# mLSTM steps as one pipelined step each, every second projection group, with PSUM bank 3 taken from the projections

## Chip, cores and metric

The kernel runs on one core of a Trainium2 chip. The metric is the device time of one execution in microseconds (us), the median of several runs. In the profile the engines are PE (matrix products), DVE, ACT, POOL (elementwise) and SP (it issues DMAs). PSUM, where PE writes and DVE and ACT read, has eight banks of 128 partitions x 512 float32.

## What is computed

One layer of a hybrid backbone over 512 latent tokens and 128 context tokens, width 1024: normalised and modulated tokens go through one wide input projection, whose columns feed three branches (neighbourhood attention, 8 heads of 64; a bidirectional mLSTM, 4 heads of 128; a gated short convolution); the branches are projected, gated, merged, and a SwiGLU feed-forward follows. The part that the change rewrites is the chunked mLSTM. For each chunk of 128 tokens, direction and head:

```
inter = b + m;  mt = max(inter, max(d));  w_int = exp(inter - mt)
s   = (q @ k.T) * exp(d - mt)                     # scores times decay
num = w_int * (q @ C) + s @ v                     # state product + score product
den = w_int * (q @ n) + sum(s)
h   = num / max(abs(den), exp(-mt))
C, n = decay * C + (wk * k).T @ v,  decay * n + sum(wk * k)
```

Attention is `softmax(q @ k.T + bias) @ v`, the projections are `h @ w_in`.

## The kernel before

Every large product is computed to float32 accuracy from float32r halves: each operand is split into a high part (ACT copies it with rounding, L1239 and its like) and a low part (DVE subtracts, L1699), and `three` (L2386 to L2390) issues three products for each 128-row slice of the contraction. So PE runs one long stream of products, in *groups*. A group fills one PSUM bank with the sum over the contraction: 24 products of 320 columns for the units q, k, mq, cc, cx, cb, gate and mo, 12 for a branch unit (br), and for mk and mv 24 products of 512 columns in four *parts* of 6. ACT or DVE then *drains* the bank, and PE may start the next group on that bank when its previous user is drained (`bank_free`, L2378).

The order of everything is a list, `PLAN`, which `make_plan` (L193) writes once; each engine walks the list in order and issues what it has to do at each step, with semaphore waits. Three things stand in that list besides the groups:

- `split` steps: for a block of weights ACT makes the high part and DVE the low part; the block's slot must first have been released by the group or part that read its previous content. Blocks of the unit `ada` are no product operands: DVE multiplies them with the condition rows in the same place (L1713).
- `side` lists: small work that is put between the groups. In `unit` (L235) one entry is taken at each of the four groups j of a unit (at j 0 and 2 alone in a br unit, other than the last), one more at j = 1 in q, k and mq units; for mk and mv (L409) an entry is taken at parts 0 and 2, and at all four parts of the last token tile. What is left at the unit `mif` is put out at once (L395), just ahead of the group `kout`, which turns the context keys.
- The side work is first attention, ten steps `na` of two units each (nine pairs; the last pair is of context heads). Step 0 of a pair: PE scores of this pair and value products of the last; DVE adds the bias, takes the maximum. ACT exponentiates the first unit in step 0, the second in step 1, where DVE divides. Step 2: PE transposes the probabilities (L2672), ACT copies them out (L1573), and the next step 0 multiplies with the values (L2657, L2661); DVE writes the result (L2107, L2110). Then the mLSTM: 20 steps `ml` of two heads (4 of the context, 16 of the latent chunks).

An ml step has two halves. `("ml", 0, n)`: PE broadcasts the row of `mpair` (L2701) and, at the first visit of a chunk and head pair, computes the scores (L2710); DVE forms the exponent (L2229), ACT scales the keys (L1609) and exponentiates (L1613), DVE multiplies (L2236). `("ml", 1, n)`, one group later: PE multiplies scores with values (L2722), queries with the state (L2724), keys with values (L2726), and turns the keys that the next first visit needs (`turn_keys`, L2528, L2536); ACT scales the state product (L1618), DVE sums and updates the state (L2244 to L2255) and normalises (L2262 to L2272). The ml steps use banks 4 to 7, called `A[0]` to `A[3]`; the projections use banks 0 to 3 in turn, but 0 to 2 from the first k unit until mif (`three_banks`), since attention keeps its value products in bank 3.

Ahead of the mLSTM stand, at units cc and cx, the steps mstat, mscan, mnat, mexp and mcols: running sums and maxima of the gates, some 23 us of small DVE operations that begin with the drain of kout (L1770) and end at L2207 and L2215. At mcols PE transposes the results (L2681), sums the chunk ends (L2685), and waits for DVE's copies of them (L2132 to L2135, semaphore `ms_rd`) before it turns the first keys:

```
                    pe.wait_ge(ms_rd, 3)
                    pe.wait_ge(act_drain, drains("A", gid("mk", 0, TT - 1)))
                    turn_keys(0)
```

After the last br unit of this stage (`("br", (2, 3))`) come eight mo groups, then products by a seven-product scheme (`wu` steps), whose sums, splits and operands DVE and ACT prepare. The feed-forward begins in the same way: `tsum` is four sums on DVE (L2305 to L2311, semaphore `ts_done` 5 to 8), and `tsplit` 0 to 3 split their results (ACT L1640, DVE L2317):

```
                    if j == 0:
                        act.wait_ge(x1_out, 16 * TT)
                        act.wait_ge(ts_done, 8)
```

Of the kernel before, what the change touches and what calls it, by code (L numbers as in the profile page):

```python
# [18 lines left out]
ALU = mybir.AluOpType  # L19
# [3 lines left out]
P = 128  # L23
# [169 lines left out]
def make_plan():  # L193
# [41 lines left out]
    def unit(n):  # L235
        kind, which = UNITS[n][:2]
        for j, emit in enumerate(tiles(n)):
# [14 lines left out]
            if side and (kind != "br" or j % 2 == 0 or UNITS[n][:2] == ("br", (2, 3))):  # L252
                plan.extend(side.pop(0))
# [137 lines left out]
    while UNITS[n][0] != "out":  # L391
        kind, which = UNITS[n][0], UNITS[n][1]
        if kind != "ada":
            if kind == "mif":
# [3 lines left out]
                three_banks[0] = False  # L398
# [88 lines left out]
    plan += [("tsum",), ("tsplit", 0)]  # L487
    ff_group("fg", 0, 0, 1)
    plan += [("tsplit", 1), ("wsum", NG)]
# [154 lines left out]
def program(nc, a, out, vline, gline, xline, gdram):  # L644

    ctx = ExitStack()
    with ctx:
# [279 lines left out]
        def _(sp):  # L927
# [42 lines left out]
            for step in PLAN:  # L970
# [50 lines left out]
                elif step[0] == "ml" and step[1] == 1 and ML_UNITS[step[2]][0] == CH:  # L1021
                    n = step[2]
# [195 lines left out]
        def _(act):  # L1218
# [48 lines left out]
            def drain(g):  # L1267
# [122 lines left out]
            def turned_keys(n):  # L1390
# [5 lines left out]
                nc.scalar.activation(kt, A[2][:, 0:256].rearrange("p (i t) -> p i t", i=2), ACT.Copy).then_inc(kt_rd, 1)  # L1396
# [81 lines left out]
            for step in PLAN:  # L1478
# [115 lines left out]
                elif step[0] == "ml":  # L1594
                    _, sub, n = step
                    ch, dr, hp, first, last = ML_UNITS[n]
                    b = n % 2
                    if sub == 0:
# [3 lines left out]
                        if SCORES[ch, hp][0] == n:  # L1602
                            nc.scalar.activation(scores[:, scores_held(ch, hp)],
                                                 A[1][:, 0:256].rearrange("p (i t) -> p i t", i=2),
                                                 ACT.Copy).then_inc(ml_sc, 1)
                        for i in range(2):
                            r = dr * 4 + 2 * hp + i
                            hd = 2 * hp + i
                            ins = nc.scalar.activation(kw_sb[:, b, i, :], mk[:, ch, hd * P:(hd + 1) * P], ACT.Copy,  # L1609
                                                       scale=mcols[:, ch, 2, r:r + 1])  # L1610
                        ins.then_inc(ml_kw, 1)
                        act.wait_ge(ml_dm, n + 1)
                        nc.scalar.activation(e_sb[:, b], e_sb[:, b], ACT.Exp, scale=-1.0).then_inc(ml_e, 1)  # L1613
                    if sub == 1 and ch < CH:
                        act.wait_ge(ml_b, n + 1)
# [5 lines left out]
                    if sub == 1 and n + 1 in FIRST_VISITS:  # L1621
# [64 lines left out]
        def _(dve):  # L1686
# [213 lines left out]
            def ada5_block(j):  # L1900
# [7 lines left out]
                ins.then_inc(ada5_done, 1)  # L1908

# [62 lines left out]
            for step in PLAN:  # L1972
# [248 lines left out]
                elif step[0] == "ml":  # L2221
                    _, sub, n = step
                    ch, dr, hp, first, last = ML_UNITS[n]
                    b = n % 2
                    if sub == 0:
                        dve.wait_ge(ml_a, n + 1)
                        for i in range(2):
                            r = dr * 4 + 2 * hp + i
                            ins = nc.vector.scalar_tensor_tensor(e_sb[:, b, i, :], A[0][:, i * P:(i + 1) * P],  # L2229
                                                                 mcols[:, ch, 0, r:r + 1], mask_m[:, dr, :],  # L2230
                                                                 ALU.subtract, ALU.max)
                        ins.then_inc(ml_dm, 1)
                        dve.wait_ge(ml_e, n + 1)
                        first_n = SCORES[ch, hp][0]
                        dve.wait_ge(ml_sc, sum(1 for v in SCORES.values() if v[0] <= first_n))
                        nc.vector.tensor_tensor(st_sb[:, b], scores[:, scores_held(ch, hp)], e_sb[:, b],  # L2236
                                                ALU.mult).then_inc(ml_st, 1)
                    else:
                        dve.wait_ge(ml_b, n + 1)
                        intra = A[3][:, 0:258].rearrange("p (i e) -> p i e", i=2)  # L2240
                        upd = A[1][:, 0:258].rearrange("p (i e) -> p i e", i=2)
# [620 lines left out]
```

## Time and profile before

| | |
|---|---|
| runs | 1126.8, 1127.04, 1125.51 us; median 1126.8 |
| profiled execution, own time | 1128.61 us |
| its span, first to last instruction | 1126.8 us |
| PE busy | 1105.7 us, 98% of the span |
| DVE, ACT, POOL busy | 790.6, 515.9, 90.6 us |
| mean granted PE clock | 0.996 of 2.4 GHz |
| HBM | 125 GB/s over the span |

Times in the rows are from the span's start. In a timeline a row is: start, duration, engine, line, operation, output<-inputs, shape, count, and in brackets the idle time just before it with what ended it. The ends of products are modelled and overlap the next ones, so what one costs is the distance from its start to the next start.

### The profile page before, as it was taken

The numbers are of one execution on the slowest core, as the hardware profiler recorded it, in microseconds if no ns is written. First come the engines' busy times: TensorE is split into PE (matmuls) and PEld (weight loads), VectorE is DVE, ScalarE is ACT, GpSimd is POOL, SyncE is SP. The second block draws the span as 40 slices with busy tenths as digits, with TensorE's granted clock in tenths as the row PEclk, the third lists the DMA queues.
The fourth block names the chain that finished last, engine by engine and source line by source line (L and its number), as shares of the span: only waits on it lengthen the run. The fifth ranks groups of instructions, "written<-read, shape, count | busy, mean of one in ns | idle before, by whom it ended". The sixth has DMA issues, their size and how long they took to land.

```text
span 1126.8 us, 18487 instructions
## 1 busy us (share of the span) xinstructions
PE 1105.7 (98%) x7136; PEld 1038.9 (92%) x7136; DVE 790.6 (70%) x1405; ACT 515.9 (46%) x965; POOL 90.6 (8%) x149
## 2 busy tenths in 40 slices
PE   6999999999999999999999999999999999999997
PEld 4799998789999999999999988999999999988886
DVE  5748978768675666888868637999987777633444
ACT  5534443434334333355553238555555555533431
POOL 2052322000000000210100003000000000000002
PEclk9999999998999999999999999999999999999999
DMA  9675563452531122035466345053422232425112
GB/s 361 237 233 166 182 197 90 145 144 81 83 68 57 57 72 61 20 101 181 145 222 225 120 128 179 18 168 127 149 77 76 87 139 75 125 67 183 57 38 93
DMA packets 42918, 141.78 MB, mean 126 GB/s; under 512 B 9392, under 2 KB 10960, under 8 KB 41168
## 3 DMA queue, kind: packets, MB, share of 16 engines
q1 hardware_dynamic: 38752, 131.64, 36.4%
q0 software_dynamic: 4080, 8.97, 2.5%
q8 instruction: 57, 0.93, 0.4%
q14 instruction: 29, 0.24, 0.1%
HBM read 127.93 MB, written 12.60 MB: 125 GB/s over the span
## 4 chain that ended last, share of the span: by engine, by line
PE 92%; DVE 4%; ACT 2%; issue 1%; DMA 1%; SPq 0%; POOL 0%; POOLq 0%; ACTq 0%; DVEq 0%
PE ps L2388 28%; PE ps L2390 28%; PE ps L2389 28%; PE ps L2657 1%; PE ps L2672 1%; PE ps L2722 1%; PE ps L2631 1%; PE ps L2724 1%; PE ps L2726 1%; DMA xt<-in_x_sample 1%; DVE w_lo L1699 1%; PE ps L2598 0%; PE ps L2446 0%; PE ps L2710 0%; PE ps L2632 0%
## 5 line engine op out<-in xcount | busy, mean ns | idle before, releaser
L2390 PE MATMUL ps<-h_hi,w_lo 128*128 128x320 f32 x960 | 297.6, 310 | 0.0
L2389 PE MATMUL ps<-h_lo,w_hi 128*128 128x320 f32 x800 | 248.3, 310 | 0.0
L2388 PE MATMUL ps<-h_hi,w_hi 128*128 128x320 f32 x736 | 232.1, 315 | 1.3 <-ACT mo L1336 0.8
L2390 PEld LDWEIGHTS ps<-h_hi,w_lo 128*128 128x128 f32 x960 | 181.2, 189 | 0.0
L2388 PE MATMUL ps<-w_hi,h_hi 128*128 128x512 f32 x418 | 164.8, 394 | 0.0
L2390 PE MATMUL ps<-w_hi,h_lo 128*128 128x512 f32 x418 | 162.8, 390 | 0.0
L2389 PE MATMUL ps<-w_lo,h_hi 128*128 128x512 f32 x418 | 162.8, 389 | 0.0
L2389 PEld LDWEIGHTS ps<-h_lo,w_hi 128*128 128x128 f32 x800 | 151.3, 189 | 0.1
L2388 PEld LDWEIGHTS ps<-h_hi,w_hi 128*128 128x128 f32 x736 | 139.3, 189 | 2.9 <-issue 2.2
L1699 DVE TENSOR_TENSOR w_lo<-raw,w_hi 128x1024 fp32r<-128x1024 f32 x93 | 112.5, 1222 | 40.3 <-ACT w_hi L1239 39.7
L1239 ACT ACTIVATE w_hi<-raw 128x1024 fp32r<-128x1024 f32 x93 | 96.6, 1052 | 65.3 <-PE ps L2390 60.3
L2388 PE MATMUL ps<-h_hi,w_lo 128*128 128x320 f32 x336 | 104.4, 311 | 0.8 <-ACT snap L1377 0.8
L2388 PE MATMUL ps<-tt_hi,w_hi 128*128 128x320 f32 x336 | 103.8, 309 | 0.0
L2389 PE MATMUL ps<-tt_lo,w_hi 128*128 128x320 f32 x336 | 103.8, 309 | 0.0
L2390 PE MATMUL ps<-tt_hi,w_hi 128*128 128x320 f32 x336 | 103.8, 309 | 0.0
L2389 PE MATMUL ps<-h_lo,w_lo 128*128 128x320 f32 x336 | 103.8, 309 | 0.0
L2388 PEld LDWEIGHTS ps<-w_hi,h_hi 128*128 128x128 f32 x418 | 78.5, 188 | 18.3 <-issue 2.1
L2390 PEld LDWEIGHTS ps<-w_hi,h_lo 128*128 128x128 f32 x418 | 78.5, 188 | 16.4
L2389 PEld LDWEIGHTS ps<-w_lo,h_hi 128*128 128x128 f32 x418 | 78.5, 188 | 15.7
L1746 DVE TENSOR_TENSOR h_lo<-ff,h_hi 128x1280 fp32r<-128x1280 f32 (+1 forms) x22 | 30.5, 1428 | 64.4 <-ACT h_hi L1264 64.4
L1830 DVE TENSOR_TENSOR w_hi<-raw,w_hi 128x512 fp32r<-128x512 f32 x84 | 58.0, 690 | 22.9 <-ACT w_hi L1368 22.8
L2388 PEld LDWEIGHTS ps<-h_hi,w_lo 128*128 128x128 f32 x336 | 63.1, 188 | 1.3 <-issue 1.2
(313 smaller groups left out, 2030.6 us busy)
## 6 DMA issues: line engine op xcount, KB each, us to landing
raw<-in_w_blocks SPq DMA_DIRECT2D x182, 512.0 KB, 3.9
ada<-in_w_first SPq DMA_DIRECT2D x8, 1024.0 KB, 20.2
gdram<-stage SPq DMA_DIRECT2D x8, 640.0 KB, 6.6
gt<-gdram SPq DMA_DIRECT2D x8, 640.0 KB, 5.8
xline<-x SPq DMA_DIRECT2D x5, 512.0 KB, 5.3
x<-xline SPq DMA_DIRECT2D x5, 512.0 KB, 7.7
xt<-in_x_sample SPq DMA_DIRECT2D x4, 512.0 KB, 6.4
condr<-in_cond_rows POOLq DMA_DIRECT2D x2, 1024.0 KB, 8.1
```

Source lines behind the costliest of these rows:

```text
L1239: ins = nc.scalar.activation(held(w_hi, b), raw[:, s, :], ACT.Copy)
L1699: nc.vector.tensor_tensor(held(w_lo, b), raw[:, s, :], held(w_hi, b).bitcast(F32), ALU.subtract).then_inc(lo_done, 1)
L1746: nc.vector.tensor_tensor(h_lo[:, o2 + k:o2 + k + n, :], ff[:, k0 + k:k0 + k + n, :], h_hi[:, o2 + k:o2 + k + n, :].bitcast(F32), ALU.subt ...
L1830: nc.vector.tensor_tensor(v[:, 512:1024], summand(w, q), v[:, 0:512].bitcast(F32), ALU.subtract).then_inc(flo_done, 1)
L2388: nc.tensor.matmul(dst, wh, xh, start=first, stop=False, skip_group_check=resumed)
L2389: nc.tensor.matmul(dst, wh, xl, start=False, stop=False, skip_group_check=resumed)
L2390: return nc.tensor.matmul(dst, wl, xh, start=False, stop=last, skip_group_check=resumed)
L2631: nc.tensor.matmul(dst[:, 0:256], q, kk, start=True, stop=True)
L2657: ins = nc.tensor.matmul(dst[:, 0:P], src, pt[:, b, i, c * P:(c + 1) * P], start=(c == 0), stop=(c == 2))
L2672: ins = nc.tensor.transpose(A[2 * b + i][:, c * P:(c + 1) * P], sx[:, b, i, c * P:(c + 1) * P], ident)
L2722: ins = nc.tensor.matmul(A[3][:, pr], st_sb[:, b, i, :], mv[:, ch, hd, :], start=True, stop=True)
L2724: ins = nc.tensor.matmul(A[0][:, pr], mq[:, hd, tok(ch)], cl[:, r, :], start=True, stop=True)
```

## The change

- The two halves of neighbouring ml steps are put together. `("ml", n)` for n = 0 to 20 holds, on PE, the turning of the next keys, the broadcast and scores of step n (`ml_scores`), then the products of step n - 1 (`ml_values`); on DVE the exponent of n, the state update of n - 1 (`ml_state`), the score product of n, the sum and normalisation of n - 1 (`ml_sum`); on ACT the parts that go with them.
- Broadcast, scores and turned keys get banks of their own: A[2] for the broadcast, bank 3 for scores and turned keys. For that the projections use three banks until the mo groups.
- One entry of `side` is taken at groups 0 and 2 of a unit (0 alone in a br unit other than the last) in place of every group.
- At mcols the first keys are turned ahead of the small transposes, and PE no longer waits there for `ms_rd`.
- In the feed-forward, tsplit 1 comes before tsplit 0, and each waits for its own sum, not for all four.
- The mo drains wait for `ml_b`, the last products, in place of `ml_h`, the last normalisation.

```
@@ make_plan
-            if side and (kind != "br" or j % 2 == 0 or UNITS[n][:2] == ("br", (2, 3))):
+            if side and (j == 0 or kind != "br" and j == 2 or UNITS[n][:2] == ("br", (2, 3)) and j == 2):
                 plan.extend(side.pop(0))
...
                 for s in side:
                     plan.extend(s)
                 side = []
-                three_banks[0] = False
                 group("kout", n)
...
             elif kind == "mo" and which == 0:
                 assert not side
+                three_banks[0] = False
                 gate_stretch()
...
             for s in range(len(ML_UNITS)):
-                side += [[("ml", 0, s)], [("ml", 1, s)]]
+                side.append([("ml", s)])
+            side.append([("ml", len(ML_UNITS))])
...
-    plan += [("tsum",), ("tsplit", 0)]
+    plan += [("tsum",), ("tsplit", 1)]
     ff_group("fg", 0, 0, 1)
-    plan += [("tsplit", 1), ("wsum", NG)]
+    plan += [("tsplit", 0), ("wsum", NG)]
@@ ACT
-                    act.wait_ge(ml_h, len(ML_UNITS))
+                    act.wait_ge(ml_b, len(ML_UNITS))
...
-                    if j == 0:
+                    if j == 1:
                         act.wait_ge(x1_out, 16 * TT)
-                        act.wait_ge(ts_done, 8)
+                    act.wait_ge(ts_done, (7, 5, 8, 6)[j])
@@ DVE
+                        ins.then_inc(ml_dm, 1)
+                    if n:
+                        ml_state(n - 1)
+                    if n < len(ML_UNITS):
...
                                                 ALU.mult).then_inc(ml_st, 1)
+                    if n:
+                        ml_sum(n - 1)
@@ PE
+            def ml_scores(n):
+                ch, dr, hp, _, _ = ML_UNITS[n]
+                if n:
+                    pe.wait_ge(ml_dm, n)
+                else:
+                    pe.wait_ge(ms_rd, 3)
+                    pe.wait_ge(stat_rd, 1)
+                    pe.wait_ge(pair_rd, 1)
...
+            def ml_values(n):
...
+                pe.wait_ge(ml_st, n + 1)
+                pe.wait_ge(ml_kw, n + 1)
+                if n:
+                    pe.wait_ge(ml_c, n)
...
                 elif step[0] == "mcols":
+                    turn_keys(0)
                     pe.wait_ge(stat_rd, 2)
...
-                    pe.wait_ge(ms_rd, 3)
-                    pe.wait_ge(act_drain, drains("A", gid("mk", 0, TT - 1)))
-                    turn_keys(0)
                 elif step[0] == "ml":
+                    if step[1] + 1 in FIRST_VISITS:
+                        turn_keys(step[1] + 1)
+                    if step[1] < len(ML_UNITS):
+                        ml_scores(step[1])
+                    if step[1]:
+                        ml_values(step[1] - 1)
```

What the order becomes, engine by engine, at three places.

PE at the end of mv, before the change (the last products of mv, then kout's transposes; the last attention products came ten parts of mv earlier):

```order
L2388 MATMUL ps<-w_hi,h_hi 128x512
L2389 MATMUL ps<-w_lo,h_hi 128x512
L2390 MATMUL ps<-w_hi,h_lo 128x512
L2388 MATMUL ps<-w_hi,h_hi 128x512
L2389 MATMUL ps<-w_lo,h_hi 128x512
L2390 MATMUL ps<-w_hi,h_lo 128x512
L2474 MATMUL ps<-cst,nak 128x128 x4
L2388 MATMUL ps<-h_hi,w_hi 128x320
```

and now (L2731 transposes the last pair's probabilities, L2720 multiplies them with the values, L2488 is kout):

```order
L2404 MATMUL ps<-w_hi,h_lo 128x512
L2402 MATMUL ps<-w_hi,h_hi 128x512
L2403 MATMUL ps<-w_lo,h_hi 128x512
L2404 MATMUL ps<-w_hi,h_lo 128x512
L2731 MATMUL ps<-cst,sx 128x128 x8
L2720 MATMUL ps<-pt,vctx 64x128 x8
L2488 MATMUL ps<-cst,nak 128x128 x4
L2402 MATMUL ps<-h_hi,w_hi 128x320
```

The last steps of attention, which had products of mv behind them, stand with none between each other and kout.

ACT in the same place, before (L1562 exponentiates, L1310 drains mv, L1573 copies the transposed probabilities, L1239 splits weights, L1577 belongs to mstat):

```order
L1573 ACTIVATE pt<-ps 128x768 x2
L1562 ACTIVATE sx,small<-sx,small 128x128 x4
L1310 ACTIVATE mv<-ps 128x4x128
L1562 ACTIVATE sx,small<-sx,small 128x128 x4
L1310 ACTIVATE mv<-ps 128x4x128
L1573 ACTIVATE pt<-ps 128x2x256 x2
L1310 ACTIVATE mv<-ps 128x4x128 x2
L1239 ACTIVATE w_hi<-raw 128x1024 x2
L1310 ACTIVATE mv<-ps 128x4x128
L1239 ACTIVATE w_hi<-raw 128x1024
L1577 ACTIVATE stat_114<-stat_113 36x640
```

and now (L1563, L1311, L1574, L1240 and L1578 are the same operations):

```order
L1574 ACTIVATE pt<-ps 128x768 x2
L1563 ACTIVATE sx,small<-sx,small 128x128 x4
L1240 ACTIVATE w_hi<-raw 128x1024
L1563 ACTIVATE sx,small<-sx,small 128x128 x4
L1240 ACTIVATE w_hi<-raw 128x1024
L1311 ACTIVATE mv<-ps 128x4x128
L1240 ACTIVATE w_hi<-raw 128x1024
L1574 ACTIVATE pt<-ps 128x2x256 x2
L1578 ACTIVATE stat_114<-stat_113 36x640
```

A split has come between the two units' exponentials, and two splits and the last drain of mv stand directly ahead of the copy of the probabilities.

PE at mcols, before (last transposes of the gate statistics, the sum of chunk ends, the first keys, then the group cx):

```order
L2681 MATMUL ps<-cst,ib 128x36
L2681 MATMUL ps<-cst,lf 128x36
L2681 MATMUL ps<-cst,stat_114 128x36
L2681 MATMUL ps<-cst,stat_119 128x36
L2685 MATMUL ps<-ends,parity 128x32
L2536 MATMUL ps<-cst,mk 128x128 x2
L2388 MATMUL ps<-h_hi,w_hi 128x320
```

and now (the first keys, L2554, ahead of the transposes):

```order
L2402 MATMUL ps<-h_hi,w_hi 128x320
L2403 MATMUL ps<-h_lo,w_hi 128x320
L2404 MATMUL ps<-h_hi,w_lo 128x320
L2554 MATMUL ps<-cst,mk 128x128 x2
L2741 MATMUL ps<-cst,ib 128x36
L2741 MATMUL ps<-cst,lf 128x36
L2741 MATMUL ps<-cst,stat_114 128x36
L2741 MATMUL ps<-cst,stat_119 128x36
L2741 MATMUL ps<-cst,ib 128x36
```

The keys' transposes have left the place behind L2685.

## Rows read from the trace of the kernel before

**Rows 1.** The page: busy time of PE.
```profile
PE 1105.7 (98%) x7136; PEld 1038.9 (92%) x7136; DVE 790.6 (70%) x1405; ACT 515.9 (46%) x965; POOL 90.6 (8%) x149
```
**Rows 2.** Waits of PE, whole span: total us, times, longest.
```profile
PE ps L2598 <- DVE xt L1983: 9.2, 2, 8.3
...
PE ps L2388 <- ACT snap L1377: 0.8, 1, 0.8
```
**Rows 3.** Timeline of PE: the last attention pair, then kout.
```profile
210.41 1.26 PE L2635 MATMUL ps<-nak,naq 64*128 64x128 f32 x16
...
213.07 0.50 PE L2388 MATMUL ps<-w_hi,h_hi 128*128 128x512 f32 x1
...
221.39 1.03 PE L2672 MATMUL ps<-cst,sx 128*128 128x128 f32 x8
...
225.10 1.09 PE L2661 MATMUL ps<-pt,vctx 128*64 128x128 f32 x16
...
239.86 0.60 PE L2474 MATMUL ps<-cst,nak 128*128 128x128 f32 x4
240.80 0.39 PE L2388 MATMUL ps<-h_hi,w_hi 128*128 128x320 f32 x1 [0.34 <-ACT mv L1310]
```
**Rows 4.** Timeline of PE: the last but one pair, in the last tile of mk.
```profile
197.78 0.71 PE L2631 MATMUL ps<-nak,naq 64*128 64x256 f32 x4
...
205.95 0.52 PE L2672 MATMUL ps<-cst,sx 128*128 128x128 f32 x3 [0.73 <-DVE sx L2122]
```
**Rows 5.** Timeline of ACT, same place: a split between the pair's two exponentials.
```profile
202.62 1.06 ACT L1239 ACTIVATE w_hi<-raw 128x1024 fp32r<-128x1024 f32 x1 [0.57 <-PE ps L2390]
203.59 0.60 ACT L1562 ACTIVATE sx<-sx,small 128x384 f32<-128x384 f32 x1
```
**Rows 6.** Timeline of DVE: a low part; last pair's division; its output.
```profile
203.72 1.23 DVE L1699 TENSOR_TENSOR w_lo<-raw,w_hi 128x1024 fp32r<-128x1024 f32 x1 [0.76 <-ACT w_hi L1239]
...
218.65 0.87 DVE L2122 TENSOR_SCALAR sx<-sx,small 128x128 f32<-128x128 f32 x4
...
226.24 0.76 DVE L2110 COPY att<-ps 128x256 f32<-128x256 f32 x2 [4.31 <-PE ps L2661]
```
**Rows 7.** Timeline of ACT: first and last of the last unit's exponentials; copy of its probabilities.
```profile
216.70 0.39 ACT L1562 ACTIVATE sx<-sx,small 128x128 f32<-128x128 f32 x1
...
218.14 0.19 ACT L1562 ACTIVATION_READ_ACCUMULATOR sx<-sx,small 128x1 f32 x1
...
222.14 1.08 ACT L1573 ACTIVATE pt<-ps 128x512 f32<-128x512 f32 x2
```
**Rows 8.** Timeline of PE: mcols and the group behind it.
```profile
266.23 0.25 PE L2681 MATMUL ps<-cst,ib 36*128 36x36 f32 x1 [0.56 <-DVE mnat L2207]
...
268.99 0.69 PE L2536 MATMUL ps<-cst,mk 128*128 128x128 f32 x2 [1.10 <-DVE dec L2135]
...
269.74 0.47 PE L2389 MATMUL ps<-h_lo,w_hi 128*128 128x320 f32 x1
```
**Rows 9.** Windows: length, PE, PEld, DVE, ACT, POOL busy, PE clock, DMA share, GB/s.
```profile
264.70:268.10 3.40, 2.63 (x29) 2.25 (x27) 3.36 (x8) 2.39 (x4) 0.00 (x0) 1.00 0.17 69
268.10:271.50 3.40, 2.51 (x10) 2.51 (x11) 3.26 (x11) 1.78 (x3) 0.00 (x0) 0.50 0.53 154
```
**Rows 10.** Timeline of DVE: drain of kout; drains of the first two cx groups.
```profile
242.78 0.69 DVE L1770 COPY sx<-ps 128x512 f32<-128x512 f32 x1
...
267.54 0.87 DVE L1781 TENSOR_TENSOR cu<-ps,cu 128x320 f32<-128x320 f32 x2
```
**Rows 11.** Timeline of PE: second half of the last ml step.
```profile
442.12 0.31 PE L2390 MATMUL ps<-bo_hi,w_lo 128*128 128x320 f32 x1
442.52 0.49 PE L2722 MATMUL ps<-mv,st_sb 128*128 128x129 f32 x2
```
**Rows 12.** Windows, columns as above: one ml step, a conv, and their groups.
```profile
327.60:336.70 9.10, 9.10 (x69) 9.10 (x68) 7.65 (x19) 3.13 (x8) 0.00 (x0) 1.00 0.21 63
```
**Rows 13.** Timeline of DVE: the first tsplit of the feed-forward.
```profile
717.11 2.98 DVE L2317 TENSOR_TENSOR tt_lo<-h,tt_hi 128x1280 fp32r<-128x1280 f32 x2 [1.40 <-ACT tt_hi L1640]
```

More of the change, by code:

```diff
@@ L1020, in _ @@
                     load_bias(sp, br0_in, 0)
-                elif step[0] == "ml" and step[1] == 1 and ML_UNITS[step[2]][0] == CH:
-                    n = step[2]
+                elif step[0] == "ml" and 1 <= step[1] <= 4:
+                    n = step[1] - 1
                     _, dr, hp, _, _ = ML_UNITS[n]
@@ L1594, in _ @@
                 elif step[0] == "ml":
[L1595 to L1598, printed above, removed]
+                    n = step[1]
+                    if n < len(ML_UNITS):
+                        ch, _, hp, _, _ = ML_UNITS[n]
                         act.wait_ge(ml_a, n + 1)
@@ L1620, in _ @@
                         ins.then_inc(ml_tmp, 1)
-                    if sub == 1 and n + 1 in FIRST_VISITS:
+                    if n < len(ML_UNITS):
+                        ch, dr, hp, _, _ = ML_UNITS[n]
+                        for i in range(2):
+                            r = dr * 4 + 2 * hp + i
+                            hd = 2 * hp + i
+                            ins = nc.scalar.activation(kw_sb[:, n % 2, i, :], mk[:, ch, hd * P:(hd + 1) * P], ACT.Copy,
+                                                       scale=mcols[:, ch, 2, r:r + 1])
+                        ins.then_inc(ml_kw, 1)
+                    if n + 1 in FIRST_VISITS:
                         turned_keys(n + 1)
@@ L2221, in _ @@
                 elif step[0] == "ml":
[L2222 to L2225, printed above, removed]
+                    n = step[1]
+                    if n < len(ML_UNITS):
+                        ch, dr, hp, _, _ = ML_UNITS[n]
                         dve.wait_ge(ml_a, n + 1)
@@ L2232, in _ @@
                         ins.then_inc(ml_dm, 1)
+                    if n:
+                        ml_state(n - 1)
+                    if n < len(ML_UNITS):
+                        ch, _, hp, _, _ = ML_UNITS[n]
                         dve.wait_ge(ml_e, n + 1)
                         first_n = SCORES[ch, hp][0]
[L2235 to L2236 removed]
+                        dve.wait_ge(ml_sc, sum(1 for v in FIRST_VISITS if v <= first_n))
+                        nc.vector.tensor_tensor(st_sb[:, n % 2], scores[:, scores_held(ch, hp)], e_sb[:, n % 2],
@@ L2533, in turn_keys @@
                     pe.wait_ge(kt_rd, o)
+                    pe.wait_ge(ml_sc, sum(1 for v in FIRST_VISITS if v < n - 1))
+                else:
+                    pe.wait_ge(na_out, len(NA_UNITS))
+                    pe.wait_ge(act_drain, drains("A", gid("mk", 0, TT - 1)))
                 for i in range(2):
                     hd = 2 * hp + i
-                    ins = nc.tensor.transpose(A[2][:, i * P:(i + 1) * P], mk[:, ch, hd * P:(hd + 1) * P], ident)
+                    ins = nc.tensor.transpose(ps[:, 3, 256 + i * P:256 + (i + 1) * P], mk[:, ch, hd * P:(hd + 1) * P], ident)
@@ new lines, in ml_values @@
+            def ml_values(n):
+                ch, dr, hp, _, last = ML_UNITS[n]
+                b = n % 2
+                pe.wait_ge(ml_st, n + 1)
+                pe.wait_ge(ml_kw, n + 1)
+                if n:
+                    pe.wait_ge(ml_c, n)
+                else:
+                    pe.wait_ge(fills, 3)
+                    pe.wait_ge(act_drain, drains("A", gid("mv", 0, TT - 1)))
+                for i in range(2):
+                    hd = 2 * hp + i
+                    r = dr * 4 + hd
+                    pr = slice(i * 129, (i + 1) * 129)
+                    ins = nc.tensor.matmul(A[3][:, pr], st_sb[:, b, i, :], mv[:, ch, hd, :], start=True, stop=True)
+                    if ch < CH:
+                        ins = nc.tensor.matmul(A[0][:, pr], mq[:, hd, tok(ch)], cl[:, r, :], start=True, stop=True)
+                    if ch == CH or not last:
+                        ins = nc.tensor.matmul(A[1][:, pr], kw_sb[:, b, i, :], mv[:, ch, hd, :], start=True, stop=True)
+                ins.then_inc(ml_b, 1)
```

151 lines of the change are left out of this document (60 added, 91 removed).

## The prediction

> **What bounds the kernel.** I read the page first: PE is busy 98% of the span [rows 1], so only what PE does, waits for, or does at a slow clock can move the end. Of the 21.1 us in which it is not busy, 9.2 lie at the start, where the tokens are loaded [rows 2]. Next, the timeline of PE around the ml steps, since the change rewrites them. It shows a dense stream: a half step begins at the very distance at which one product follows another, with two exceptions, of which one is [rows 11]: the product at 442.12 is followed only 0.40 us later, where the others of its kind follow at 0.15. With the slower first product behind the wait, each of the two costs 0.35 us. So pipelining the steps can give back 0.7 us and no more. What else there is to win lies at mcols: PE waits for DVE's last sums, later for its copy of the chunk ends [rows 8], and from 268.1 the granted clock is 0.50, that is 1.2 GHz of 2.4 [rows 9]; it stays there up to 274.9. What PE did just ahead was small transposes with waits between them. One wait more is in the feed-forward, for a snapshot of ACT [rows 2], behind a DVE that was held up 1.40 us by the first tsplit [rows 13].
>
> **The parts of the change**, against the profiled execution (1128.61 us, span 1126.8). The median of the runs shown is 1126.8, 1.8 below; I apply the sum to it.
>
> *1. The end of attention: +3.4.* The new rule takes three entries a unit in place of five from q, k and mq, so attention runs two pairs late and its last two entries are put out directly behind the last product of mv, ahead of kout. Nothing then covers the chain PE, DVE, ACT, PE. I lay it out from t, the start of the last pair's scores, with durations of the same pair where it stands now.
> - PE: scores and the other pair's value products take 2.66 (210.41 to 213.07) [rows 3]; 18 products of mv, at 0.23 each with a slower first, 4.2: ready at t+6.87.
> - ACT and DVE now have a split between the two units' exponentials. The pair before shows that order today: the split starts 4.84 after its scores, the second exponentials 0.97 after that [rows 4, 5]. The context pair's PE work is 0.4 shorter, so its second exponentials start at t+5.40; they take 1.63 (216.70 to 218.33) [rows 7], to t+7.03. DVE's low part takes 1.2 [rows 6], to about t+6.7, its two divisions 1.1 each (0.87 and a reciprocal) [rows 6], to t+7.8 and t+8.9.
> - PE transposes the first unit at t+7.85 (idle 1.0), the second at t+8.95 (idle 0.7), 0.4 each (0.79 for both, 221.39 to 222.18).
> - ACT has two splits (1.06 each) [rows 5] and a drain (0.5) ahead of the copy of 1.08 [rows 7]: it is through at t+10.7. PE multiplies at t+10.83 (idle 1.5).
> - DVE's output starts 1.14 after these products (225.10 to 226.24) and takes 0.76 [rows 3, 6]. kout starts at t+12.83, 0.98 after the products' 1.02 are out.
>
> The idle sum is 4.15. Against it stands that the bank behind kout is free (kout took 0.94 for 0.45 of work, with a wait for mv's drain) [rows 3], and two slow re-entries into the stream of 0.1 are saved: +3.45. Today's wait of [rows 4] stays, for another pair.
>
> *2. mcols: -2.2.* kout's drain started 1.98 us after the next group did, since DVE still had splits to do [rows 3, 10]; in the new order these are done in the idle time above, and the drain starts 0.15 after. The chain of small operations up to L2207 is DVE's own, so it ends 1.8 earlier against PE, and the wait of 0.56 at 266.23 is gone. The keys' transposes take 0.22 and no longer wait 1.10. Between the last cx product (265.37) and the next group's first (0.41 ahead of 269.74) lie 3.96 us; left are 0.15 for the product, 0.22, the small transposes' 1.27 and 0.12 for the chunk ends. The new bank rule makes this group wait for the drain of cx 0, done at 267.98 today [rows 10]; moved by 1.8 it ends 0.9 ahead of PE. -2.2.
>
> *3. The clock: 0.* The 24 products behind mcols took 6.12 us where others take 3.60: the half clock costs 2.5. In the new order 1.6 us of small work stand there and the waits are gone. Nothing in the rows shows such a place; I choose the full clock, and the other outcome is a rival. But at part 1 there now stand 6 us in which PE works 2.3 and idles 4.1, more empty than 264.7 to 268.1 [rows 9], which was followed by the half clock. I take the same stretch, at kout and the first cc group: +2.5, bounded by 0 and by 3.4, half of the 6.8 us that the slow clock lasted.
>
> *4. ml steps: -0.7 for the waits, +0.9 at mo.* The products are the same ones, and where the small ones stand costs nothing: the stream before and behind is dense. Three banks: a group may start when the group three earlier is drained, so a drain has the time of two groups, 7.2 us, or 3.6 in a br unit. In one step period of 9.1 us DVE is busy 7.65 [rows 12]; with its waits for ACT's exponential, some 0.7, I reckon 8.4 of 9.1, the same work in either order. Behind an ml step in a br unit, the first drain ends by my sum of durations 6.1 after PE's first product of the step and is wanted at 7.3. Covered, but with little left. At the first mo group the rotation changes from three to four, and it falls on the bank of the very last br group. DVE drains that one behind the last ml sum (1.7) and another drain (0.8): about 0.9 after PE asks for it. Today that bank is not the next one, and nobody waits. I take +0.9, between 0.5 (a drain and its signals alone) and 2.0.
>
> *5. tsplit: -1.2.* ACT starts with the block that the first sum ends, so DVE need not wait 1.40 for it [rows 13]. DVE is without a gap from there to the snapshot's wait. Of 1.4 I take 1.2: the waits of PE there are 0.93 us at 732.34, 0.37 and 0.12, and the snapshot can't come before its product. Bounds 0 and 1.4.
>
> *6. Queues.* SP now waits for `ml_c` n one step later, ahead of a load whose block is needed four blocks on; state copies land well before their buffers are used again. 0.
>
> Sum: 3.45 - 2.2 + 0 - 0.7 + 0.9 - 1.2 = **+0.3**, 1127.1 us. The bounds of the terms, set off against each other, leave 1125.3 to 1129.4 for this case.
>
> **The rivals.** A measurement of this kernel can tell about 0.2%, 2.25 us, from no change.
> - *No half clock at kout.* The transposes and value products that stand in the gap keep the clock up. In favour: 203.2 to 206.7 has a wait and transposes and kept its clock. Against: it had 2.7 busy of 3.4. The sum is then -2.2: 1124.6.
> - *The chain of part 1 is shorter*, because DVE and ACT run ahead where attention is thinned out, and hide half of it: 1.7 less, with or without the clock: 1122.9 to 1125.4.
> - *Slower: three banks do not cover DVE.* The 8.4 of 9.1 us leave 0.7. If one more wait of DVE for ACT of 0.5 to 0.8 comes into each step, the drain wanted two groups later is late, and PE stops once in each of four br units and at two conv steps, 0.7 us each: +4.2, 1131.3. It decides when the first br drain ends over 7.3 us behind the ml step's start; I have it at 6.1.
> - *Slower: the half clock at both places.* mcols' 1.6 us of small transposes still bring it down: +2.5, 1129.6.
> - *Half clock behind every late drain.* In the trace the attention units run on three banks with no clock below 1.0, so I give this little; one stretch more costs 2.5, two +5.3 in all: 1132.1. The Trainium skill, TensorE: Matmul & The Clock Gate, section "A second HAM failure mode: psum-queue depth-cycling", says that small idles of PE between groups that cycle through PSUM banks can make its clock swing between the two levels; by it fewer banks would be slower. The rows so far do not bear it out for 0.2 us idles.
>
> **How the numbers follow.** Forecast 0.50; no half clock 0.14; shorter chain 0.11; three banks 0.12; both places 0.09; every late drain 0.04. Faster by over 0.2%: all of the shorter chain, half of no half clock, 0.02 of the forecast: 0.20. Slower: three banks, the last rival, two thirds of both places, 0.03 of the forecast: 0.25. The rest, 0.55, is within 0.2%. The range goes from 1123.4 to 1130.6; it leaves out the fast end of the shorter chain and the far ends of the slower rivals.
>
> **What would show it.** In the new profile: waits of PE for sx, pt and att ahead of kout, together 4.1 us, idle ended by DVE, ACT, DVE; a stretch at clock 0.50 at kout and none at mcols, where the distance from cx to cx is 1.8 us; a wait of 0.9 of the first mo group for the last br drain; the snapshot's wait under 0.3; no wait of PE in the ml steps. I am wrong if PE waits for drains between cc and mo, if the gap at kout is under 2.5 us or over 6, or if the clock is 1.00 from start to end.

## The result, and the profile after

| | before | changed |
|---|---|---|
| median of the runs | 1126.8 us | 1132.47 us (1131.46 to 1132.88, 5 runs) |
| ratio | | 1.0045, 95% interval 1.0033 to 1.0056 |
| profiled execution, own time and span | 1128.61, 1126.8 | 1132.47, 1130.7 |
| PE busy | 1105.7 | 1106.7 |

The changed kernel is slower by 5.7 us, 0.45%. The prediction had 1127.1 and a range that ends at 1130.6: it was wrong, and the loss lies outside its range.

The waits of PE over the whole span of the changed kernel, the answer to [rows 2]:

```profile
...
PE ps L2402 <- ACT w_hi L1240: 2.0, 1, 2.0
PE ps L2731 <- DVE sx L2169: 2.0, 3, 0.8
...
PE ps L2720 <- ACT pt L1574: 1.1, 1, 1.1
PE ps L2488 <- DVE att L2157: 0.9, 1, 0.9
PE ps L2402 <- issue: 0.8, 1, 0.8
PE ps L2402 <- ACT mo L1337: 0.8, 1, 0.8
PE ps L2402 <- DVE gt L1806: 0.7, 1, 0.7
```

Four of these I had foreseen (`sx`, `pt` and `att` ahead of kout, and `gt`, the last br drain ahead of the first mo group). The one for `w_hi` and the one for "issue" I had not. The kernel before waits for `mo` as well. The waits for the snapshot, for the chunk ends (`dec`) and for `mnat` are gone.

To see where the time went, one lays the two traces beside each other at the same product: both run the same 6102 large products in the same order, so the start of the n-th is the same point of the work. From there to the next mark, in us:

| stage of PE | before | changed |
|---|---|---|
| first large product to the start of cc (all of attention, kout) | 216.64 | 225.71 |
| cc and half of cx, up to behind mcols | 28.53 | 28.28 |
| the group behind mcols, with the first scores | 6.61 | 4.32 |
| ml stage up to its last groups | 164.57 | 164.05 |
| last groups, first mo group | 8.29 | 8.84 |
| mo, gate scheme, out, first part of the feed-forward | 296.13 | 294.67 |
| the rest | 375.67 | 375.66 |

The whole loss is in the first line, +9.07; everything behind gives back 4.0. From the first large product to the last that is 5.1 us. (The spans differ by 3.9 alone, since in this execution the changed kernel had its first large product 1.2 us earlier, at 22.93 in place of 24.16.) In that first line lies this, in the timeline of PE of the changed kernel, in the second mq unit:

```profile
147.39 0.31 PE L2404 MATMUL ps<-h_hi,w_lo 128*128 128x320 f32 x1
149.72 0.40 PE L2402 MATMUL ps<-h_hi,w_hi 128*128 128x320 f32 x1 [2.02 <-ACT w_hi L1240]
```

A product that should follow at 147.54 comes at 149.72. ACT is named as the releaser, but ACT's split of this block (144.61, 1.05 long) had been done for 4 us; the group also waits for the low part. The timeline of DVE at the same place:

```profile
132.97 1.22 DVE L1702 TENSOR_TENSOR w_lo<-raw,w_hi 128x1024 fp32r<-128x1024 f32 x1
138.31 0.96 DVE L2133 TENSOR_TENSOR sx<-ps,bm 128x768 f32<-128x768 f32 x1 [4.13 <-PE ps L2691]
139.31 0.95 DVE L2136 TENSOR_REDUCE small<-sx 128x2 f32<-128x768 f32 x1
...
142.42 1.55 DVE L1716 SCALAR_TENSOR_TENSOR prod_a<-raw,condr_a 128x1024 f32<-128x1024 f32 x1
...
143.90 1.75 DVE L1716 SCALAR_TENSOR_TENSOR raw<-raw,condr_a 128x1024 f32<-128x1024 f32 x1
...
148.41 1.21 DVE L1702 TENSOR_TENSOR w_lo<-raw,w_hi 128x1024 fp32r<-128x1024 f32 x1
149.54 0.15 DVE L2166 RECIPROCAL small<-small 128x2 f32<-128x2 f32 x1
```

DVE stood idle for 4.13 us, since the next thing in its order was the bias of a pair whose scores PE had yet to make. Then came, in a row: bias and maxima of two units, a short output copy, two blocks of condition rows (L1716, two operations each), and last the low part that PE wants, done at 149.6: 11.3 us from the start of the bias. From there to 147.54 PE had 9.2 us of work, 7.1 of them the two groups from 140.40 on; the difference is the wait of 2.18. A smaller wait of the same kind stands at 101.99 (0.98; "issue" in the waits; PE goes on at 103.12, as DVE's low part ends). In the kernel before neither place has a wait.

Windows of the changed kernel (length, PE, PEld, DVE, ACT, POOL busy, PE clock, DMA share, GB/s), behind that wait and around kout:

```profile
146.80:150.20 3.40, 1.38 (x10) 1.14 (x9) 3.36 (x8) 2.39 (x4) 0.00 (x0) 0.96 0.63 178
150.20:153.60 3.40, 3.40 (x15) 3.40 (x15) 3.29 (x6) 1.17 (x2) 0.00 (x0) 0.53 0.75 269
243.80:247.20 3.40, 2.07 (x20) 1.46 (x17) 2.23 (x3) 1.29 (x3) 0.00 (x0) 0.75 0.50 169
247.20:250.60 3.40, 2.70 (x11) 2.73 (x12) 2.08 (x9) 0.00 (x0) 0.66 (x2) 0.50 0.52 186
```

Both places are followed by the half clock: 1.6 us more for the products behind the first, 1.7 for those behind kout and 1.0 within the tail. The tail itself, in PE's timeline:

```profile
241.21 0.39 PE L2404 MATMUL ps<-w_hi,h_lo 128*128 128x512 f32 x1
242.37 0.66 PE L2731 MATMUL ps<-cst,sx 128*128 128x128 f32 x4 [0.77 <-DVE sx L2169]
243.49 0.66 PE L2731 MATMUL ps<-cst,sx 128*128 128x128 f32 x4 [0.47 <-DVE sx L2169]
245.23 1.73 PE L2720 MATMUL ps<-pt,vctx 128*64 128x128 f32 x16 [1.09 <-ACT pt L1574]
247.90 1.09 PE L2488 MATMUL ps<-cst,nak 128*128 128x128 f32 x4 [0.94 <-DVE att L2157]
248.64 0.61 PE L2402 MATMUL ps<-h_hi,w_hi 128*128 128x320 f32 x1
```

DVE, DVE, ACT, DVE, as forecast. The bracketed waits sum to 3.3 us, since the modelled ends of the products run into them; by the starts of the products PE idles 3.95. At mcols, the place of [rows 8, 9], nothing is waited for any more:

```profile
275.03 0.38 PE L2554 MATMUL ps<-cst,mk 128*128 128x128 f32 x2
275.34 0.25 PE L2741 MATMUL ps<-cst,ib 36*128 36x36 f32 x1
...
276.92 0.41 PE L2402 MATMUL ps<-h_hi,w_hi 128*128 128x320 f32 x1
```

### The profile page after: what moved, and what is told of

It reads as the page before. It is cut to its first block, busy times and chain, and to the rows that moved or that the text cites. A ratio compares the mean times of both kernels' runs of the same rounds, so it can differ in the third digit from the quotient of the medians.

```text
span 1130.7 us, 18479 instructions
## 1 busy us (share of the span) xinstructions
PE 1106.7 (98%) x7136; PEld 1039.7 (92%) x7136; DVE 789.4 (70%) x1405; ACT 516.0 (46%) x965; POOL 91.1 (8%) x149
## 4 chain that ended last, share of the span: by engine, by line
PE 96%; DMA 1%; ACT 1%; issue 1%; DVE 1%; SPq 0%; POOLq 0%; POOL 0%; ACTq 0%
PE ps L2402 30%; PE ps L2404 29%; PE ps L2403 29%; DMA ada<-in_w_first 1%; PE ps L2716 1%; PE ps L2731 1%; PE ps L2690 1%; PE ps L2591 1%; PE ps L2593 1%; PE ps L2595 1%; PE ps L2572 0%; PE ps L2460 0%; PE ps L2691 0%; PE ps L2787 0%; ACT w_hi L1240 0%
## 5 line engine op out<-in xcount | busy, mean ns | idle before, releaser
L2404 PEld LDWEIGHTS ps<-h_hi,w_lo 128*128 128x128 f32 x960 | 181.5, 189 | 0.0
L1240 ACT ACTIVATE w_hi<-raw 128x1024 fp32r<-128x1024 f32 x93 | 96.9, 1054 | 61.7 <-PE ps L2404 54.9
L1378 ACT ACTIVATE snap<-ps 128x320 f32<-128x320 f32 x80 | 34.9, 437 | 63.6 <-PE ps L2404 63.6
```

The lines of the kernel that those rows point to most:

```text
L1240: ins = nc.scalar.activation(held(w_hi, b), raw[:, s, :], ACT.Copy)
L1378: nc.scalar.activation((gsnap if w < NG else snap)[:, i, :], wbank(w, 1 if i == 2 else 0), ACT.Copy).then_inc(fsnap, 1)
L2404: return nc.tensor.matmul(dst, wl, xh, start=False, stop=last, skip_group_check=resumed)
```

## Experiments

The theory after this reading, A: the loss comes wholly from attention's thinned rate, by four pieces: the late low parts (3.2 us), the half clock behind them (1.6), the tail (3.5 to 4.5), the half clock at kout (up to 2.7, which is 1.0 within the tail and 1.7 behind it). Rivals: three banks, or the pipelined steps. Each run below stands beside runs of the kernel before on the same chip; in three sets their medians were 1127.99, 1127.95 and 1127.47 us, from 62 runs between 1124.65 and 1129.73.

### 1. Attention's old rate in the changed kernel

```
-            if side and (j == 0 or kind != "br" and j == 2 or ...
+            if side and (kind in ("q", "k", "mq") or j == 0 or kind != "br" and j == 2 or ...
```

> The changed kernel with one rule undone: in q, k and mq units attention takes its side entries at every group again, as before the change; the pipelined ml steps, banks, mcols and feed-forward stay changed. Theory A (the loss is all in the thinned attention: waits of PE for late low parts at 101.99 and 147.39, together 3.2 us, the half clock behind the second, 1.6, the uncovered tail ahead of kout, 4.45, and the half clock at kout, 1.7): all four vanish; kout's drain is late again against PE, so that mcols loses up to 1.8. The time is 1132.5 - 10.9 + 0 to 2 = 1121.6 to 1123.6, faster than both kernels. Rival B (the loss is in three banks or in the pipelined steps): it stays at or above 1128. Rival C (the half clock of mcols comes back, since the wait for the last mnat does): 1124 to 1126.

Measured: 1124.79 us, ratio to before 0.9970 (0.9959 to 0.9981). 7.7 us below the changed kernel, by one condition, and 3.2 faster than before: what is left of the change is a gain when taken together. In its trace all four pieces are gone. Of the expectations C came true, in its time and its condition: at mcols the wait for `mnat` is back, and behind it the half clock (the group there takes 5.86 us, against 6.61 before and 4.32 in the changed kernel). Waits of PE in 260 to 272:

```profile
PE ps L2742 <- DVE mnat L2255: 0.9, 1, 0.9
PE ps L2403 <- DVE cu L1785: 0.2, 1, 0.2
```

### 2. The thinned rate alone in the kernel before

```
-            if side and (kind != "br" or j % 2 == 0 or ...
+            if side and (j % 2 == 0 or kind not in ("q", "k", "mq", "br") or ...
```

> The kernel before with the thinned side rule in q, k and mq units alone; ml steps in two halves as before, mcols and feed-forward as before. Theory A: the waits for low parts, their half clock and the tail come with this rule alone: +3.2 + 1.6 + 4.5 + 1.7 = +11, less what mcols gains from a kout drain that is no longer late (0 to 3): 1134 to 1138. Rival B: within 2 us of the kernel before.

Measured: 1132.84 us, ratio 1.0047 (1.0035 to 1.0060), below the range I gave. The same waits stand at the same products, so the rule does it without anything else of the change: the first line of the table is 224.16 (before 216.64). But behind mcols the group takes 4.08 (before 6.61), and the wait of 2.18 us at 149.57 was this time not followed by the half clock (the one at kout was):

```profile
148.60:152.00 3.40, 1.38 (x10) 1.14 (x9) 3.37 (x7) 2.32 (x5) 0.00 (x0) 1.00 0.71 173
152.00:155.40 3.40, 3.40 (x24) 3.40 (x25) 3.30 (x7) 1.61 (x2) 0.00 (x0) 1.00 0.77 280
```

I had put both half clocks into the sum as if each came with its wait.

### 3. Splits ahead of the attention entry, rate still thinned

In outline, for the kinds q, k and mq:

```
             for j ...
-                plan.extend(side.pop(0))
                 split_to(...)
+                plan.extend(side.pop(0))
```

> The changed kernel with the order within a step altered: in q, k and mq units the weight splits and the condition rows stand ahead of the attention entry of that place, not behind it; the rate stays thinned. Theory A1 (PE waited at 147.39 because DVE idled 4.1 us, then had bias, maxima, two condition blocks and the low part in a row, 11.3 us for 7.0 us of cover): DVE does the two condition blocks in its idle time, the wait of 2.2 and the half clock behind it (1.6) vanish, the tail stays: 1132.5 - 3.8 = 1128.7, or 1127.7 if the wait at 101.99 goes too. Rival (the block's load is late, whatever DVE does first): 1132.5, with the wait where it was.

Measured: 1128.77 us, ratio to before 1.0004 (0.9993 to 1.0014), 3.7 below the changed kernel. The block's load was never late. Timeline of DVE, the same blocks as above:

```profile
136.66 1.22 DVE L1719 SCALAR_TENSOR_TENSOR raw<-raw,condr_a 128x1024 f32<-128x1024 f32 x1
...
138.86 0.96 DVE L2136 TENSOR_TENSOR sx<-ps,bm 128x768 f32<-128x768 f32 x1 [0.97 <-PE ps L2694]
...
146.24 1.23 DVE L1705 TENSOR_TENSOR w_lo<-raw,w_hi 128x1024 fp32r<-128x1024 f32 x1 [3.19 <-ACT w_hi L1243]
```

The condition blocks have gone into DVE's idle time, which is 0.97 us ahead of the bias in place of 4.13, and now DVE waits for ACT ahead of the low part, not PE for DVE. Both waits of PE and the half clock are gone; the tail is as it was. This settles the wait at 147.39: it was the order on DVE.

### 4. Three banks in the kernel before

```
-                three_banks[0] = False
-                group("kout", n)
+                group("kout", n, bank=3)
             elif kind == "mo" and which == 0:
+                three_banks[0] = False
```

> The kernel before, in which the projections keep three banks up to the mo groups, nothing else changed (kout in bank 3). Theory A (three banks cover DVE's load; only the first mo group waits for the last br drain): +0.5 to +1.0, 1127.3 to 1127.8, perhaps 1 more at the mcols place, where a group now waits for cx 0's drain. Rival (drains come too late at conv and br steps, or the small idles lower the clock): +3 or more.

Measured: 1129.00 us, ratio 1.0008 (0.9999 to 1.0018): +1.0, not clear of nothing by the interval. PE's waits between 275 and 476:

```profile
PE ps L2388 <- DVE gt L1803: 0.7, 1, 0.7
```

One wait, ahead of the first mo group. Three banks cover the drains of the whole ml stage, and the clock is 1.00 in the window from 275 to 450. Ahead of it the trace shows something that I had not asked for: kout, in a bank of its own, no longer waits for mv's drain (0.6 less), and the wait for `mnat` at mcols grows from 0.56 to 1.14. The chain of gate statistics is DVE's, and what PE saves ahead of it, it waits at its end.

### 5, 6. The waits at mo

```
-            group("mo", UNIT_OF[("mo", m)], f, h)
+            group("mo", UNIT_OF[("mo", m)], f, h, bank=(len(groups) + 3) % 4)
```

on top of experiment 1 (5), and with it, at the first products of the gate scheme (6):

```
-                    pe.wait_ge(act_drain, drains("A", gid("mo", 1, 1, 1)))
+                    pe.wait_ge(act_drain, drains("A", gid("mo", 1, 0, 1)))
+                elif w == 0 and q == 1:
+                    pe.wait_ge(act_drain, drains("A", gid("mo", 1, 1, 1)))
```

> The changed kernel with attention's old rate (attn_rate_back), and the mo groups moved one bank on, so that the first of them falls on bank 3, which no group has used for long, in place of bank 0, which the last br group has just filled. Theory A (the 0.83 us that PE stands ahead of the first mo group is the drain of that bank, and only that): the wait is gone and nothing takes its place: attn_rate_back - 0.8. Rival (DVE is late there whatever the bank, and the next group or the scheme's first product waits instead): no change.

> As mo_in_bank3, and the first product of the gate scheme waits only for the drain of the mo group in its own bank, its second product for that of the last mo group, where both kernels wait for the last at the first product (0.92 us of PE at 476.81 before, 0.91 after). If that wait is the whole cause: attn_rate_back - 1.7, 1123.1. If ACT, which has a split ahead of that drain, is late by more than one product of the scheme (1.8 us): between that and attn_rate_back - 0.8.

Measured: 1123.69 us, ratio 0.9964 (0.9952 to 0.9977), and 1123.42 us, ratio 0.9958 (0.9946 to 0.9971). In the trace of 5, PE waits between 440 and 480 once,

```profile
PE ps L2403 <- ACT mo L1338: 0.8, 1, 0.8
```

and in that of 6 not at all. Both waits are gone with nothing in their place: 0.83 and 0.91 us by the traces. The medians fell by 1.1 and then by 0.3; their intervals (some 1.4 us to either side) resolve neither step.

### 7. The keys behind the small transposes

```
-                    turn_keys(0)
                     pe.wait_ge(stat_rd, 2)
...
+                    pe.wait_ge(ms_rd, 3)
+                    turn_keys(0)
```

on top of experiment 1, with ACT's copy of the keys moved likewise.

> attn_rate_back with the first keys turned behind the small transposes again, after PE has waited for the copies of the chunk ends, as before the change. Theory: PE waits 1.1 us for these copies once more, +1.1; if the half clock behind mcols lasts longer for it (24 products in place of 11), up to +2.3. Rival: the keys' place is worth nothing, since PE would wait for cx 0's drain anyway: 0.

Measured: 1126.55 us, ratio 0.9990 (0.9981 to 0.9999), 1.8 above experiment 1. Waits of PE in 260 to 272:

```profile
PE ps L2741 <- DVE mnat L2255: 1.1, 1, 1.1
PE ps L2555 <- DVE dec L2183: 1.1, 1, 1.1
```

The 1.1 for `dec` is back, as forecast, and the wait for `mnat` is a little longer, since the keys' transposes no longer cover part of it. Between the last cx product and the next are 4.55 us in place of 3.29, so the place is worth 1.3; the slow clock behind it ended earlier in this execution and hid 0.5 of that.

### 8. The new tsplit order alone in the kernel before

The diff's lines on `tsum`, `tsplit`, `ts_done` and `t_hid`, nothing else.

> The kernel before with the new order of tsplit alone. Theory: the waits of PE of 0.93 us for ACT's snapshot and of 0.37 for DVE's operand go: -1.3, 1125.5 to 1126.7 against 1126.8 to 1128.0 of the kernel before. Rival: another wait for a low part takes their place, -0.5 or less.

Measured: 1126.31 us, ratio 0.9990 (0.9981 to 0.9999), 1.6 below before. PE's waits of 0.93 and 0.37 are gone. The windows of this run are worth more than that:

```profile
264.00:267.40 3.40, 2.85 (x32) 2.59 (x30) 3.32 (x9) 2.80 (x5) 0.00 (x0) 1.00 0.27 107
267.40:270.80 3.40, 2.29 (x17) 2.18 (x17) 3.29 (x11) 1.60 (x3) 0.00 (x0) 1.00 0.50 154
```

Up to mcols this is the kernel before, with its two waits there (0.6 for `mnat`, 1.1 for `dec`), and this time the clock stayed at 1.00, where [rows 9] have 0.50.

### 9, 10. The tail alone, and the changed kernel again

Experiment 1, with the last pair's steps held back in mv so that its end is the changed kernel's, entry for entry:

```
-                        if side and (j % 2 == 0 or t == TT - 1):
+                        if side and (j % 2 == 0 or t == TT - 1) and (kind == "mk" or t == TT - 1 or len(side) > 6):
```

> attn_rate_back with the last pair's steps held back in mv, so that its end is the changed kernel's (the last transposes and value products directly ahead of kout), while attention in q, k and mq keeps the old rate. Theory A (this tail by itself costs 4.4 us of idle and 0 to 2.2 of half clock, and gives back about 1 at mcols, whose wait for mnat goes): attn_rate_back + 3.4 to + 5.5, 1128.2 to 1130.3. Rival (the tail is cheap by itself, and the changed kernel's loss was in the backlog of low parts): + 2 at most.

> The changed kernel itself, beside the others on the same chip: 1131.5 to 1133, about 7.7 above attn_rate_back; with tail_alone it splits this sum in two: what is above tail_alone is the thinning in q, k and mq (3.2 of waits and 0 to 1.6 of half clock).

Measured: 1127.38 us, ratio 1.0003 (0.9992 to 1.0014), and for the changed kernel 1132.49, ratio 1.0044 (1.0030 to 1.0059), its first result once more. The tail costs 2.6 by the medians as they are, and 3.1 when each is first compared with the kernel before in its own set. My expectation began at 3.4; with intervals of 1.2 us to either side that is not a clear miss. The waits of PE around kout are the changed kernel's:

```profile
PE ps L2732 <- DVE sx L2170: 1.2, 2, 0.8
PE ps L2721 <- ACT pt L1575: 1.1, 1, 1.1
PE ps L2489 <- DVE att L2158: 0.9, 1, 0.9
```

but by the stages, +4.36 up to cc stands against -1.24 in the stage to mcols and -1.54 behind it. In the 4.36 are 0.8 of this run's own: at 206.95 PE waits 1.5 for a low part, where experiment 1 waits 0.7 for `sx`. The -1.24 is the wait for `mnat` (0.9) and the one for `cu` (0.2) behind it, both gone: what one idles ahead of kout, one does not idle at mcols. The -1.54 is the half clock behind mcols in experiment 1, and that did not have to come: the trace of experiment 5, with the same order and wait there, has 4.33 us for the same group. The other 5.1 of the 7.7 us, measured in one set, are the late low parts and their clock, 4.8 by the traces.

The second profile of the changed kernel has the same waits in the same places (the one near 102 is 1.30 there, not 0.98), and the half clock behind one of them only. Windows behind the wait for the low part, and at kout:

```profile
150.20:153.60 3.40, 1.37 (x10) 1.40 (x10) 3.29 (x9) 2.44 (x3) 0.00 (x0) 1.00 0.72 253
153.60:157.00 3.40, 3.40 (x15) 3.40 (x14) 3.37 (x5) 1.06 (x1) 0.00 (x0) 0.51 0.75 214
245.40:248.80 3.40, 1.85 (x22) 1.30 (x20) 2.91 (x5) 2.20 (x4) 0.00 (x0) 1.00 0.46 146
248.80:252.20 3.40, 2.46 (x20) 2.45 (x19) 2.47 (x9) 0.00 (x0) 0.66 (x2) 1.00 0.73 281
```

### 11. kout's drain first

On top of experiment 6, the last split of mv's stage moves behind kout.

> both_waits_off with the last weight split of mv's stage put behind kout, so that DVE drains kout at once and the chain of gate statistics begins 1.2 us earlier against PE. Theory: PE's wait of 0.98 for the last mnat ahead of the small transposes goes, the one of 0.19 behind them at most in part: -1.0 to -1.2 on both_waits_off, 1122.3, and where the half clock followed, 0 to 1.3 more. Rival (ACT's steps of the chain bind, not DVE's start, or the split is then late for cc): 0 or a loss.

Measured: 1123.17 us, ratio 0.9956 (0.9940 to 0.9972). Against experiment 6 that is no difference that can be measured. PE's waits around mcols:

```profile
PE ps L2746 <- DVE mnat L2257: 0.4, 1, 0.4
...
PE ps L2405 <- DVE cu L1787: 0.2, 1, 0.2
```

The wait for `mnat` went from 0.98 to 0.37. That is 0.6, a third of what it might have been: against PE, DVE starts to drain kout not 1.2 but 1.8 us earlier (0.78 in place of 2.57 behind the first cc product). What binds the rest was not tried. It has the lowest median of all, 4.3 us below the kernel before.

## Why the prediction was wrong, point by point

| term | predicted | in the traces |
|---|---|---|
| 1. tail ahead of kout | +3.45 | +3.46 at full clock, +1.0 where it fell inside |
| 2. mcols | -2.2 | -1.9 |
| 3. clock at mcols, at kout | -2.5, +2.5 | -2.5, +1.7 behind kout (and the 1.0 above); at kout 0 in the second profile |
| 4. ml waits, first mo group | -0.7, +0.9 | -0.55, +0.83 |
| 5. tsplit | -1.2 | -1.55 |
| not in the sum: late low parts | 0 | +3.2 (3.5 in the second profile) |
| not in the sum: clock behind them | 0 | +1.6 |

**The step that failed** is in part 1, which reads from "The new rule takes three entries a unit in place of five from q, k and mq" that its only cost is the tail. Of the moved entries I costed where the last ones land, and put at nothing, without a reason, what the earlier ones do on the way. They changed DVE's order in the q, k and mq units: a bias that waits for PE's scores now stands ahead of the condition blocks and of the low part of a block that PE needs two groups later. I had read DVE at the tail, at mcols and in the ml stage, and never against the due times of the low parts in the 120 us where the rule acts most. Those 4.8 us (3.2 and 1.6) are most of the 5.4 that lie between the forecast and the result. With them the sum comes to +5.1, which is what the traces have between the first and the last large product. That the two agree so well is in part luck: the terms for mcols, tsplit and the ml waits are each off by 0.15 to 0.35, in both directions. Experiment 3 took 3.7 us away by the order alone, and experiment 1, with the tail, all 7.7. (Product by product, against the second profile of the changed kernel, what experiment 3 removes is 5.1.)

**The tail** was right in its chain and size. From the last product of mv (243.72 in the second profile) to the first of cc (250.16) are 6.44 us; less the product's 0.23 and 2.26 of work that is 3.95 of idle, for which I had 4.15; less the 0.49 that kout lost before, 3.46. (The forecast took off 0.2 more, for two re-entries.)

**mcols** came 0.3 short, because the new end costs 2.04 where I had 1.76. **tsplit** exceeded my bound of 1.4 a little: besides the waits of 0.93 and 0.37 PE had lost 0.25 in a small wait and in slow re-entries, and these went as well.

**The first mo group**: the size was right, the reason was not. DVE was not behind: it had been idle for 0.23 us when it drained the br group, as the group ended. The wait is simply that of two groups in a row in one bank, which I had put down as the lower bound, at 0.5. It is 0.83, so that I came near by luck.

```profile
453.50 0.49 DVE L1806 SCALAR_TENSOR_TENSOR gt<-gt,ps 128x320 f32<-128x320 f32 x1 [0.23 <-PE ps L2404]
```

**The clock** I had added like a duration. The runs show that it isn't one: the same waits at the same products were followed by 1.2 GHz in one execution and not in another, at kout (changed kernel, twice), at mcols ([rows 9] against experiment 8), and behind the wait of 2.2 us (0.53 in the changed kernel, 1.00 in experiment 2). Counted over the 13 traces, the half clock followed in 2 of 3 at that wait, in 2 of 5 at the tail ahead of kout, in 6 of 8 at mcols where waits of 0.6 to 2.3 us together are left, and in none of 5 at mcols where at most 0.3 is waited. What decides it no run here was made to show. For such a place the honest term is a range from 0 to its 1.3 to 2.7 us. It is also much of why one kernel's runs differ by 5 us: of the 62 runs of the kernel before, the 15 with a mean clock of 0.996 have a median of 1128.4 us, the 14 with 0.998 or 0.999 one of 1125.6. Another part is the start: the first large product stood between 22.9 and 25.2 us in the 13 traces.

**The rivals.** Three banks not covering DVE is refuted by experiment 4 and by the changed kernel itself, in which DVE has 7.74 busy of 9.10 in a window of one ml step (323.92 to 333.02; 7.65 in that of [rows 12]) and PE doesn't wait. The rival of the half clock behind late drains named 1132.1 us, close to the result, but no drain was late: that is a coincidence. Its page, the Trainium skill, TensorE: Matmul & The Clock Gate, section "A second HAM failure mode: psum-queue depth-cycling", speaks of frequent small idles of PE between groups. In the changed kernel projections went round three banks for some 365 us, and the clock fell in that time only behind the wait of 2.2 us and at kout; the frequent small idles did not come about, so no run here tests the rule. None of the signs that I had set for being wrong was seen either (late drains from cc to mo, a gap at kout under 2.5 or over 6, a clock of 1.00 throughout). None of the rivals was the one that happened: I had asked of DVE whether it is fast enough to drain, and not whether its order lets it prepare.

## What to carry to other kernels

If a planner's rule changes how often side work is taken, check at every block that an engine prepares for PE when it is ready and when it is due, over the whole stretch in which the rule acts, not at its end alone. An in-order engine that idles ahead of an operation waiting for PE, with preparation queued behind it, is the sign: put the work that waits for nobody first. And keep a stall that may bring the half clock out of the sum as a fixed number: take the stall for certain and the clock as a range.

## What the runs showed of the hardware that was not expected

- The half clock behind a given stall is not reproducible: see above; of two profiles of one kernel one shows it at kout and the other doesn't.
- DVE and POOL slowed each other. In the stretch ahead of the wait, DVE's products of condition rows took 1.55, 1.75 and 1.57 us, beside two elementwise operations of POOL that took 2.78 together:

```profile
143.46 2.78 POOL L1118 TENSOR_TENSOR bm<-braw,cst 128x256 f32<-128x256 f32 x2
```

In experiment 3, where DVE did this work in 133.0 to 137.9 with POOL idle, each took 1.22, and POOL's pair, later, 1.44. Three stretched operations add 1.2 us to the 11.3, about half of PE's wait. No run was made for this, but all 13 traces agree: the 41 to 45 such products in each that met no elementwise operation of POOL took 1.21 to 1.23 us, those that met one 1.29 to 1.75. One POOL operation of this kind took 0.72 to 0.75 by itself or beside DVE's TENSOR_REDUCE, 0.84 to 0.95 beside its TENSOR_SCALAR, and up to 1.72 beside the products of condition rows. So it depends on which operation of DVE it meets.
- A wait put down to ACT was one for DVE. It was put down to ACT's split, which had ended 4 us earlier; only the timeline of DVE, whose low part ends 0.1 us ahead of PE's start, showed the one that decided.
